# VectorE's low weight split moved ahead of the head-pair scores and of the gating in a fused first block

## The reference

```python
p_rw, q, c_kv, iq, ik, iw, gates = _split(xn @ w_in[l], IN_SPLITS)
y_a = _rwkv7_time_mix(p_rw, ...) @ w_branch_rwkv[l]
y_b = _dsa_attention(q, c_kv, iq, ik, iw, ...) @ w_branch_dsa[l]
g_a, g_b = jnp.split(jax.nn.sigmoid(gates), N_BRANCHES, axis=-1)
h = h + (g_a * y_a + g_b * y_b) @ w_out[l]
```

## Time and profile before

| What | Value |
|---|---|
| median of 3 runs | 3791.88 us |
| the profiled execution's own time | 3793.68 us |
| its span, first to last instruction | 3791.9 us |
| TensorE matmuls busy | 3572.6 us (94%), 20488 instructions |
| VectorE busy | 2152.5 us (57%) |
| ScalarE busy | 1740.7 us (46%) |
| GpSimd busy | 345.5 us (9%) |
| mean granted TensorE clock | 0.97 |

### The profile page before, as it was taken

How to read it: one execution, slowest core, us unless ns; L and a number is a source line. 1 busy time by engine, 2 the same in 40 slices (tenths; PEclk the granted TensorE clock), 3 DMA queues, 4 the chain that set the end, 5 groups by cost and what they waited for, 6 DMA issues and landing times. The chain is left out here.

```text
span 3791.9 us, 51414 instructions
## 1 busy us (share of the span) xinstructions
PE 3572.6 (94%) x20488; PEld 3043.3 (80%) x20488; DVE 2152.5 (57%) x2869; ACT 1740.7 (46%) x2595; POOL 345.5 (9%) x217
## 2 busy tenths in 40 slices
PE   7899999888889999999999999996999998897999
PEld 6677777667679999888899998885888886786777
DVE  4676545644455477555544465555688864355454
ACT  4454333423334487444444444444655543333762
POOL 0000000000049800000000000000122210000000
PEclk9999999999999999999999999998999999899999
DMA  5454233454534555555555665553433334354344
GB/s 205 143 198 161 102 120 136 160 200 144 173 139 177 181 172 178 185 213 190 190 202 187 232 228 212 191 190 140 170 139 141 131 138 164 114 188 147 134 144 155
DMA packets 111176, 636.40 MB, mean 168 GB/s; under 512 B 18762, under 2 KB 24682, under 8 KB 39192
## 3 DMA queue, kind: packets, MB, share of 16 engines
q1 hardware_dynamic: 104840, 619.80, 45.9%
q0 software_dynamic: 5296, 13.15, 1.1%
q10 hardware_dynamic: 864, 1.09, 0.1%
HBM read 609.01 MB, written 21.54 MB: 166 GB/s over the span
## 5 line engine op out<-in xcount | busy, mean ns | idle before, releaser
L223 DVE TENSOR_TENSOR lo_w<-ring,hi_w 128x1024 fp32r<-128x1024 f32 x500 | 612.2, 1224 | 1021.9 <-ACT hi_w L217 1014.2
L217 ACT CAST hi_w<-ring 128x1024 fp32r<-128x1024 f32 x540 | 568.8, 1053 | 975.3 <-DMA ring<-in_wstream 947.3
L225 DVE TENSOR_TENSOR lo_w<-ring,hi_w 128x1024 fp32r<-128x1024 f32 x500 | 611.7, 1223 | 0.0
L1924 PE MATMUL PS<-hi_x,hi_w 128*128 128x256 f32 x2048 | 576.5, 281 | 5.5 <-POOL lo_w L225 3.0
L1924 PE MATMUL PS<-hi_x,lo_w 128*128 128x256 f32 x2048 | 579.9, 283 | 0.0
L1924 PE MATMUL PS<-lo_x,hi_w 128*128 128x256 f32 x2048 | 571.3, 279 | 0.0
L218 ACT CAST hi_w<-ring 128x1024 fp32r<-128x1024 f32 x540 | 564.7, 1046 | 0.0
L1950 PE MATMUL PS<-hi_w,lo_g 128*128 128x512 f32 x1024 | 405.5, 396 | 0.0
L1950 PE MATMUL PS<-hi_w,hi_g 128*128 128x512 f32 x1024 | 401.5, 392 | 2.0 <-issue 2.0
L1950 PE MATMUL PS<-lo_w,hi_g 128*128 128x512 f32 x1024 | 399.4, 390 | 0.0
L1924 PEld LDWEIGHTS PS<-hi_x,hi_w 128*128 128x128 f32 x2048 | 388.9, 190 | 6.0 <-ACT GG L2054 3.4
(11 more groups left out here) (515 smaller groups left out, 5825.1 us busy)
## 6 DMA issues: line engine op xcount, KB each, us to landing
ring<-in_wstream SPq DMA_DIRECT2D x540, 1024.0 KB, 4.8
other_G<-staged SPq DMA_DIRECT2D x32, 256.0 KB, 6.1
hot<-other_G SPq DMA_DIRECT2D x8, 1024.0 KB, 6.8
x<-in_x SPq DMA_DIRECT2D x2, 2048.0 KB, 8.5
gates_dram<-gst POOLq DMA_DIRECT2D x8, 512.0 KB, 4.7
x_dram<-x SPq DMA_DIRECT2D x2, 2048.0 KB, 10.9
x<-x_dram SPq DMA_DIRECT2D x2, 2048.0 KB, 9.3
prev<-RKV POOLq DMA_DIRECT2D x6, 508.0 KB, 5.5
```

Of the source, the lines that this page charges most:

```text
L217: a.copy(hi_w[s][:, 0:HALF], ring[s][:, 0:HALF]).then_inc(S(f"hi{s}"), 1)
L223: v.tensor_tensor(lo_w[s][:, 0:HALF], ring[s][:, 0:HALF], hi_w[s][:, 0:HALF].bitcast(F32), ALU.subtract)
L225: v.tensor_tensor(lo_w[s][:, HALF:UNIT], ring[s][:, HALF:UNIT], hi_w[s][:, HALF:UNIT].bitcast(F32), ALU.subtract)\
L1924: m = nc.tensor.matmul(PS[:, s, 0:T], wa[s][:, k * P:(k + 1) * P], xa[:, k, :], start=(k == 0 and p == 0), stop=(k == KC - 1 and p == 2))
```

## The change

In VectorE's loop over the units the low split of unit u + 3 is moved up by two places: ahead of `maxima` of a pair and ahead of `gated`. It acts where one of these two stands in the iteration: at the 16 units of `PAIR`, and at u = 77, 79, 81, 83, 85 and 87 (at 89 and 91 there is no unit u + 3 to split). Everything else, and every other engine's order, stays as it is. No instruction is added or taken away.

```diff
                 if u == 3:
                     norm_c()
+                if u + 3 < LASTU:
+                    lo(u + 3)
                 if u in PAIR:
                     maxima(PAIR[u])
                 if u >= WIN and (u - WIN) % 2:
                     gated(u)
-                if u + 3 < LASTU:
-                    lo(u + 3)
                 if u in (11, 13):
                     scores((u - 11) // 2)
                 if u == 12:
```

## The result

The changed kernel takes 3832.3 us (median of 4 runs, 3829.7 to 3835.8), against 3791.9 us before: ratio 1.0102, 95% interval [1.0089, 1.0116]. It is slower by about 40 us, which is the side that was forecast, but more than the 25.9 us of the sum and above the range's end of 3829. The profiled execution took 3835.75 us; its span is the one shown here.

The account below looks back on a forecast made before the run. TensorE, 94% busy, was taken to be bound by its waits for VectorE's steps. Pairs +20.6 us (4.0 + 1.3 + 9.3 + 6.0) and gating +5.3 gave +25.9, so 3817.8 us against 3791.9; range 3806 to 3829.

Parts of the forecast that it names:

- what bounds, and the sign: Whole kernel: TensorE, busy 94%, waits for VectorE's steps, never the low split; 0.7% slower, chance of slower 0.86.
- some 14: Line 796: TensorE's waits grow from 5 to this many, about 1.5 us each in pairs 11 to 14.
- the chain in a row: Wide pairs 11 to 14: high split through next transpose runs serially, 9.12 us against 7.67, 1.5 us new wait each.
- the lock at pair 2: Pair 2, line 1424: VectorE's pass no longer meets GpSimd's row copy, 0.3 us instead of 3.41; `pn` 2.7 us earlier.
- The rival that counted this gain and a landing that stays: Pairs 0 to 5: row copy's landing does not move, these pairs give about -1.2 us; total +20.7 us, chance 0.2.
- the row copy's landing: GpSimd's copy, awaited before pair 5: landing moves 2.3 us with its issue, leaving TensorE +4.0 us behind pair 5.
- The gain counted as swallowed: Pair 2's 2.7 us gain, taken to disappear in the longer wait at pair 5.
- pair 5's 1.1: Pair 5: its own chain gets 1.1 us longer, with 2.27 + 1.76 + 0.88 in a row in place of 3.9.
- the 5.9 of u = 87: Gating at u = 87: late refill delays the low split, so TensorE gets the first bank 5.9 us later.
- the gating: u = 77 to 87: +2.3, 0, -2.3, -2.3, 0, +5.9, plus 1.7 us clock loss: +5.3 us.
- the landing's ends: TensorE behind pair 5: -1.2 to +1.7 us if the row copy's landing stays, +4.0 if it moves with its issue.
- chances of the clock: Rival: clock drops unhidden at pairs 8, 9, 10 and 5, 1.7 us each; +33 us, 3825, chance 0.13.

Follow-up runs that it names:

- the first profile: Profiled execution of the changed kernel itself, nothing else changed against it: 3835.75 us; the kernel's median is 3832.3 us.
- the second: Profile from running the unaltered changed kernel again, among the follow-up kernels; that session measured 3830.9 us, 1.0101 of the kernel before.
- the run with pairs 6 to 15: Kernel before with the low split early at pairs 6 to 15 only: 3815.5 us, 1.0052 of the kernel before.
- the pairs alone: Kernel before with the low split early at all head pairs, the gating keeping its old order: 3823.1 us, 1.0080 of the kernel before.
- pair 2 back: Changed kernel with the low split put behind again at pair 2 (u = 18) only: 3824.6 us, 1.0081 of the kernel before.
- alone: Kernel before with the low split early at pair 2 (u = 18) only: 3801.7 us, 1.0020 of the kernel before.
- held: Kernel before with the low split early at pair 2 only, plus 10 scratch additions (5 us) ahead of pair 2's division: 3796.1 us in one run.
- high split first: Changed kernel with ScalarE's high split ahead of the transposed pair's copy where two pair units follow each other: 3821.8 us, 1.0079 of the kernel before.
- the gating alone: Kernel before with the low split early at the gating only, the pairs keeping their old order: 3802.9 us, 1.0025 of the kernel before.

## Why the prediction was wrong in size

**Right: what bounds, and the sign.** Moved-up work was work that nobody waited for, and VectorE's steps behind it were the ones TensorE waits for. Waits at line 796 grew from 5 to 12 in the first profile and 13 in the second, where some 14 were forecast.

**Right: the chain in a row.** Per pair, from the starts of the transposes: pair 1 +0.6 (on record +0.6), pair 2 -2.9 (-2.7), pair 4 +0.7 (+0.6), pair 7 +1.3 (1.3), pair 8 +3.1 (2.8), pair 9 +2.5 (2.4), pair 10 +2.1 (2.1), pairs 11 to 14 +6.3 (6.0), pair 15 +1.9 (2.0). Pair 6 added 0.5 in this profile, 0.1 in the second and nothing in the run with pairs 6 to 15, so that the sum left it out was right. The runs with the pairs alone and with pairs 6 to 15 alone repeat the same amounts pair by pair.

**Right: the lock at pair 2.** Line 1424 fell from 3.41 to 0.29 us in each kernel that has the low split early there. "SBUF — State Buffer", section "Who interferes with whom", in the Trainium skill gives the reason: in a two-port mode VectorE and GpSimd shut each other out. The trace agrees: 3.41 us beside the copy's issue, 0.29 us ahead of it. The rival that counted this gain and a landing that stays (3812.6) fell: the landing is what moved most.

**Wrong: the row copy's landing.** The step that failed is "If its landing moves with its issue (2.3 us)". It moved by the issue and by another 3.4 to 3.6 us, so pairs 1 to 5 cost 7.3 to 7.5 us in place of 4.0. The copy's own transfer got slower, because the shorter wait at pair 2 brings the refill of unit 20's slot up to 8 to 9 us behind the copy's issue. The gain counted as swallowed did not merely vanish: it made the landing later. Three runs show it (pair 2 back, alone, held), and so do the packets. (Two terms of the sum were rounded 0.1 us too high: pair 5's 1.1 is 1.0 by its own figures, and the 5.9 of u = 87 is 5.8.)

**Right, with one size off: the gating.** u = 77, 81, 83 and 87 did what was said (waits 10.9, 3.0, 2.8 and 5.8 us). The line

```profile
860.92 1.23 DVE L223 TENSOR_TENSOR lo_w<-ring,hi_w 128x1024 fp32r<-128x1024 f32 x1 [8.37 <-ACT hi_w L217]
...
863.20 1.28 DVE L1653 TENSOR_TENSOR mixed<-PS,ga 128x512 f32<-128x512 f32 x2
...
864.03 0.76 PE L696 MATMUL PS<-hi_w,hi_x 128*128 128x512 f32 x1 [5.78 <-DVE mixed L1653]
```

is the place u = 87, in timelines of VectorE and TensorE: the low split starts 8.4 us after VectorE was free, `gated` 2.3 us later, and TensorE goes on at 864.03; the window from 863 shows its clock at 0.50. The term was +5.3 and measured +8.6 and +4.2, the difference being where the low clock fell between u = 81 and u = 83.

**Missing: what lies outside.** The sum had nothing for the stretch behind the gating, where no instruction is changed. Both profiles have +4.7 and +5.3 us there. About 3 us of it have a place and go with the clock. From u = 91's `gated` to VectorE's first instruction of line 2160, windows with the granted clock behind the busy times; the kernel before, then the changed kernel:

```profile
848.14:1139.72 291.58, 248.43 (x1275) 211.50 (x1275) 147.94 (x303) 108.92 (x121) 43.88 (x18) 0.94 0.43 152
```

```profile
885.42:1179.91 294.49, 250.35 (x1274) 212.94 (x1275) 149.16 (x302) 108.64 (x121) 43.78 (x18) 0.92 0.42 150
```

Of the six profiles with the low split early at u = 87, five have +2.7 to +3.4 us in this stretch at a mean clock of 0.92, that is 3.4 us more lost to the low level; the sixth (high split first) has -0.9 at 0.94. The other seven beside the kernel before have -0.5 to +0.3 at 0.94. So another 3 us mostly come with the change at u = 87, by where the low clock falls behind it; that fits the gating alone, which came out above its sum. Why one kernel is spared is not shown. Behind this mark the changed kernel has +1.8 and +2.3, within what the others show (-2.8 to +5.4).

The +3.1 and +0.1 between pair 15 and u = 77 need no cause in the change: the other profiles have from -6.2 to +3.9 there, the lowest with a mean clock of about 0.96 and the highest with 0.94. The same holds for whole runs. Of 60 later runs of the kernel before, the 15 fastest (mean 3790 us) have a mean clock of 0.971, the 15 slowest (3798 us) 0.969. The eight runs of the changed kernel have 0.964 to 0.967.

So of the 14.5 us between the sum and the median, some 3.5 are the landing and some 3 the low clock behind u = 87. The rest is not traced to a step; in the first profile it stands where the low clock took more, between pair 15 and u = 77 and between u = 81 and u = 83. That it came out slower than the range is in part chance.

**The range.** 3806 to 3829 was built from the landing's ends (-1.2 to +4.0) and chances of the clock. It had no case in which a transfer gets slower through an earlier neighbour; that alone would have made 3821 us, still inside. And it took the kernel's span of one execution as exact to 0.1 us, where later runs of the very same kernel before spread over 19 us.

## What to carry to other kernels

Work that runs ahead of its need belongs behind the steps that someone waits for, not ahead of them: ask of each place which wait ends last there, since the same move cost 1.5 us at a head pair and gave 2.3 us at two places of the gating. Before moving a step up, see what it waits for itself: here another engine's order held it, and everything behind it on its own engine inherited that wait. And a shorter wait brings transfers forward; look which transfer is in flight then, because it can lose more than was gained.

## What was not expected of the hardware

- A copy of 285.8 KB from SBUF to SBUF that GpSimd issues row by row, with its small second part, was felt 23.4 to 24.7 us behind its issue where the next 1 MB refill came 13 to 14 us later, and 27.4 to 28.3 us where it came 8 to 9 us later.
- The same 421 matmuls with the same waits took 37.3, 38.7, 40.3 and 41.8 us at mean granted clocks of 1.00, 0.96, 0.92 and 0.88; which of these an execution gets changed from one run of a kernel to the next.
- A new wait of 5.8 us went with 3.4 us more lost to the low clock in the 290 us behind it, in five profiles of six, over a stretch in which no instruction was changed.
- The kernel before, whose first runs lay within 2.3 us, spread over 3784 to 3804 us in later sessions, the slower runs at the lower mean clock.
